# Input loads of an encoder block in a new order: x first, constants on the second queue, tiles 4 to 7 reordered

## The chip, the core and the metric

One NeuronCore of a Trainium2 chip runs the whole program. It has TensorE (PE, matrix products and transposes), VectorE (DVE), ScalarE (ACT), GpSimd (POOL) and SyncE (SP), which run side by side and meet at semaphores only. Loads are started by SP or ACT, each on a queue of its own, and are carried out by the same 16 DMA engines. The metric is the device time of one execution in microseconds; the time of a kernel is the median of its runs.

## The reference

One layer of an encoder in float32: 512 tokens, width 1024, hidden width 2816. The part at the start, which the change touches, is this (cut from the reference):

```python
c_act = jax.nn.silu(c)
mods = jnp.split(c_act @ w_ada[l] + b_ada[l], N_MOD, axis=-1)
sh1, sc1, g1, sh2, sc2, g2, sh3, sc3, g3 = mods
h = modulate(rmsnorm(x, norm_g[l, 0]), sh1, sc1)     # y * (1 + scale) + shift
x = x + 0.5 * g1[:, None, :] * swiglu(h, w_ffn1_in[l], w_ffn1_out[l])
```

Then come a mixer (a bidirectional HGRN2 group and a windowed attention group with a relative bias from `rel_bias` and a sink logit) and a second FFN. All of it is computed from `x`, `c` and the weights.

## The kernel before

Every float32 product is made of three products of parts rounded to a narrower format: `hi_hi`, `lo_hi` and `hi_lo`, of the weights (`w_hi`, `w_lo`) and of the modulated input (`h_hi`, `h_lo`). The input is kept transposed, as 8 tiles of 128 channels by 512 tokens. A unit is 256 columns of a weight matrix, in two banks; units 0 and 1 are the gate and the up part of the first 256 hidden channels.

The start cannot wait for all of the modulation, so it is made in pieces. The scale vector of the first norm has 1024 values, each a sum of 1024 products of `cact` (silu of c) and a column of `w_ada`. Its first quarter (tiles 0 and 1) is summed by PE: `direct_sums` (L2141) multiplies `scale_in[0]` with `cact`. The second quarter (tiles 2 and 3) is summed by PE as a row (`direct_rows`, L2151), and DVE takes the diagonal (L1448). The half for tiles 4 to 7 is summed by DVE (`scale_step`, L1384), from `scale_half`, and PE adds over partitions (`column_sums`, L2133). `shift_step` does the same for the shift. `first_factor` (L1394) makes the factor of a tile; ACT then writes `h_hi` (`first_hi`, L785) and `tmod` (`first_t`, L791), and DVE writes `h_lo` (`first_lo`, L1413). The norm itself comes from squares of `x_nat` on ACT and DVE, and `turn_xn` (L2130) transposes the normed x, `turn_x` (L2127) x itself; ACT copies the latter to `xT` (`evac_x`, L781).

The order of all this is written out by hand, one list for each engine:
- SP (L519 to L552) issues loads: `c_row`, `ident` (the identity that every transpose multiplies with), the two halves of x, `sink_r`, `table`, `relb` (for the attention bias), the first scale quarter in two halves, weights of unit 0 (tiles 0 to 3) and unit 1, the second scale quarter, `scale_half`, the rest of unit 0's weights, and, once the first sums are done (`s_mm`), the shift.
- ACT (L763 to L858) issues six small loads into `rows` (L770, L772: biases, norm gains and the like), makes `cact` (L774), squares x, and works through the tiles. The weights of unit 0 are split by ACT in two parts, at L812 and, for tiles 4 to 7, at L831.
- PE (L2117 to L2266) starts with `spin` (L2112), products of ones that nobody reads, then waits for `c_row` and `ident`, transposes c, x and `rows`, makes the sink and bias products (L2174, L2175), the direct sums, and goes through `hi_hi`, `lo_hi` and `hi_lo` of units 0 and 1 in parts of two tiles.
- DVE (L1427 to L1485) squares, scales, splits weights and makes the low parts.

PE, ACT and DVE each take their list in order; a wait in it holds all that is behind it.

Of the kernel before, what the change touches and what calls it, by code (L numbers as in the profile page):

```python
# [28 lines left out]
P = 128  # L29
TOK = 512  # L30
D = 1024
DT = D // P
# [76 lines left out]
def build(nc, x, c, w_ada, b_ada, norm_g, w_ffn1_in, w_ffn1_out, w_ffn2_in, w_ffn2_out,  # L109
# [163 lines left out]
    with ctx:  # L273
# [119 lines left out]
        def as_f32(ap):  # L393
            return ap.bitcast(f32)
# [91 lines left out]
        def _(sp):  # L486
            wa = w_ada[0].rearrange("(k p) m -> p k m", p=P)

            def load_scale(q, piece):
                sp.dma_start(scale_in[q][:, 4 * piece:4 * piece + 4, :],  # L490
                             wa[:, 4 * piece:4 * piece + 4, D + 2 * P * q:D + 2 * P * (q + 1)]
                             ).then_inc(first_ready[2 * q + piece], 16)
# [26 lines left out]
            sp.dma_start(c_row[:], c.rearrange("o (t q) -> (o t) q", q=P)).then_inc(consts_loaded, 16)  # L519
            sp.dma_start(ident[:], ident_c.ap()).then_inc(consts_loaded, 16)  # L520
            for half in range(2):
                sp.dma_start(x_nat[:, 2 * half:2 * half + 2, :],
                             x[0].rearrange("(t p) d -> p t d", p=P)[:, 2 * half:2 * half + 2, :]
                             ).then_inc(x_loaded[half], 16)
            sp.dma_start(sink_r[:], attn_sink).then_inc(bias_consts, 16)
# [3 lines left out]
            load_scale(0, 0)  # L529
            load_scale(0, 1)  # L530
            load_w(0, slice(0, 4), first_ready[6])
            load_w(1, everything, raw_ready[1])
            load_scale(1, 0)
            load_scale(1, 1)
# [3 lines left out]

            sp.wait_ge(s_mm, 1)
# [208 lines left out]
        def _(a):  # L748
# [11 lines left out]
            for f in ffns:  # L760

                a.sem_inc(f.silu, 1 if f.r else 2)
            a.wait_ge(pool_set, 3)  # L763
# [17 lines left out]
            def evac_x(d):  # L781
                a.wait_ge(x_tr, d + 1)
                sc.activation(xT[:, d, :], bank[X_BANK[d]][:], ACT.Copy).then_inc(xT_act, 1)

            def first_hi(d):  # L785
                a.wait_ge(xn_tr, d + 1)
                a.wait_ge(fac_done[0], (1, 1, 2, 2, 3, 3, 3, 3)[d])
                sc.activation(h_hi[:, d, :], bank[XN_BANK[d]][:], ACT.Copy, scale=fac[:, 0, d:d + 1]
                              ).then_inc(norms[0].hi, 1)

            def first_t(d):  # L791

                a.wait_ge(norms[0].lo, d + 1)
                sc.activation(tmod[:, d, :], bank[XN_BANK[d]][:], ACT.Copy, scale=fac[:, 0, d:d + 1]
                              ).then_inc(norms[0].t, 1)
# [5 lines left out]
            a.wait_ge(vec_step, 1)  # L801
            sc.activation(vec[:], bank[0][:, 0:P], ACT.Copy).then_inc(vec_step, 1)
            square(2)
            a.wait_ge(xsq_done, TT)
            sc.activation(rms0[:, 1, :], rms0[:, 0, :], ACT.Sqrt, bias=eps_t[:], scale=1.0 / D).then_inc(norms[0].rt, 1)
            a.wait_ge(norms[0].rinv, 1)
            sc.activation(xn[:, 0, :], x_nat[:, 0, :], ACT.Copy, scale=rms0[:, 2, 0:1]).then_inc(norms[0].rt, 1)
            evac_x(0)
            a.wait_ge(bias_mm, 1)
            sc.activation(row8[:], bank[3][0:QH, :], ACT.Copy).then_inc(rowpad_done, 1)  # L810
# [16 lines left out]
            a.dma_start(bias_rows.rearrange("(h j) -> h j", h=QH), row8[:]).then_inc(bias_stored, 16)  # L827
            evac_x(3)
            evac_x(4)
            a.wait_ge(raw_ready[0], 16)  # L830
            sc.activation(w_hi[0][:, 4 * 2 * P:], w_first[0][:, 4 * 2 * P:], ACT.Copy).then_inc(whi_done, 1)  # L831
            first_hi(4)
            first_hi(5)
            first_t(4)
            first_hi(6)
# [412 lines left out]
        def _(v):  # L1248
# [121 lines left out]
            def first_step(step, out, chunk, k, first=0):  # L1370

                if k == first:
                    ins = ve.tensor_scalar(out, chunk, cact[:, k:k + 1], None, ALU.mult)
                else:
                    v.wait_ge(s_step, step + k - first)
                    ins = ve.scalar_tensor_tensor(out, chunk, cact[:, k:k + 1], out, ALU.mult, ALU.add)
                ins.then_inc(s_step, 1)
# [6 lines left out]
            def scale_step(k):  # L1384
                if k % 4 == 0:
                    v.wait_ge(first_ready[4 + k // 4], 16)
                first_step(16, scale_acc[:], scale_half[k // 4][:, k % 4, :], k)
# [41 lines left out]
            v.wait_ge(vec_step, 2)  # L1429
            ve.tensor_scalar(modv[:, DT:2 * DT], vec[:, DT:2 * DT], 1.0, None, ALU.add).then_inc(lb_dve, 1)  # L1430
# [4 lines left out]
            for t in range(1, TT):  # L1435
                ve.tensor_scalar(xn[:, t, :], x_nat[:, t, :], rms0[:, 2, t:t + 1], None, ALU.mult).then_inc(xn_done, 1)
            v.wait_ge(lb_dve, 1)
# [7 lines left out]
            ve.tensor_tensor(w_lo[1][:], w_first[1][:], as_f32(w_hi[1][:]), ALU.subtract).then_inc(wlo_done, 1)  # L1445
            v.wait_ge(s_mm, 2)
# [3 lines left out]
            v.wait_ge(s_step, 15)  # L1450
            ve.tensor_reduce(quarter_acc[0][:, 0:2], diagonal, AX.X, ALU.add).then_inc(s_step, 1)
            v.wait_ge(s_step, 16)
# [3 lines left out]
            v.wait_ge(c_step, 2)  # L1456
            for k in range(3):
                scale_step(k)
            for k in range(3, DT):
                scale_step(k)  # L1460
# [577 lines left out]
        def _(pe):  # L2038
# [102 lines left out]
            def direct_sums(q, piece):  # L2141

                pe.wait_ge(first_ready[2 * q + piece], 16)
                for i in range(2):
                    for k in range(4 * piece, 4 * piece + 4):
                        ins = te.matmul(SCALE_SUMS[2 * q + i], scale_in[q][:, k, i * P:(i + 1) * P],
                                        cact[:, k:k + 1].to_broadcast([P, P]), start=(k == 0), stop=(k == DT - 1))
                if piece == 1:
                    ins.then_inc(s_mm, 1)
# [10 lines left out]
            spin(4)  # L2160
# [4 lines left out]
            spin(3)  # L2165
            pe.wait_ge(rows_loaded, 16 * 6)
            te.transpose(bank[0][:, 0:P], rows[:], ident[:]).then_inc(vec_step, 1)
            spin(1)
# [3 lines left out]
            pe.wait_ge(pool_set, 7)  # L2172
            pe.wait_ge(bias_consts, 48)
            te.matmul(SINK_SUM, ones[0:1, :], sink_r[:], start=True, stop=True).then_inc(sink_step, 1)  # L2174
            te.matmul(bank[3][0:QH, :], relb[:], table[:], start=True, stop=True).then_inc(bias_mm, 1)  # L2175
            pe.wait_ge(vec_step, 2)
            direct_sums(0, 0)
            direct_sums(0, 1)
            pe.wait_ge(norms[0].rt, 2)
            pe.wait_ge(xn_done, 3)  # L2180
            for d in range(3):
                turn_xn(d)
# [54 lines left out]
            hi_lo(1, (2, 3)).then_inc(first_used, 1)  # L2237
# [3 lines left out]
            column_sums(24, scale_acc, 4)  # L2241
            pe.wait_ge(xT_act, 5)
# [3 lines left out]
            for tiles in ((4, 5), (6, 7)):  # L2246
                if tiles[0] == 6:
                    pe.wait_ge(norms[0].t, 5)
                    turn_xn(7)
                hi_hi(0, tiles)  # L2250
                pe.wait_ge(wlo_done, 2)
                lo_hi(0, tiles)
                ins = hi_lo(0, tiles)
            ins.then_inc(stage_done, 1)
# [453 lines left out]
```

## Time and profile before

| | us |
|---|---|
| median of 3 runs | 1030.61 (1030.56 to 1030.64) |
| the profiled execution | 1030.24 |
| its span | 1028.4 |
| PE busy | 1020.9 (99%) |
| DVE busy | 801.9 (78%) |
| ACT busy | 507.3 (49%) |

The profile is one execution. Times are from the start of its span. A row of a timeline has the start, the time taken, the engine, the line of the kernel, the operation with its tiles, how many instructions were merged, and in brackets the idle time before it with what ended that. The profiled execution is 1.8 us longer than its span.

### The profile page before, as it was taken

Reading aid. Unit: us, or ns where it says so; the run is one execution under the profiler, and the core shown is the slowest. Engines: PE = TensorE matmul, PEld = TensorE weight load, DVE = VectorE, ACT = ScalarE, POOL = GpSimd, SP = SyncE. Lnnn points to the kernel's source line nnn. Section 1 sums busy time; section 2 is a strip of 40 time slices with the busy share of each in tenths; the row PEclk is TensorE's granted clock in tenths of the full one; section 3 lists DMA queues with packets and bytes.
Section 4 is the critical chain, followed back from the end, with each engine's and each line's share of the span. In section 5 each row is a group of like instructions: output and inputs, shape, how many; then the busy total and the mean of one; then the engine's idle time right before and its main releaser. Section 6 shows DMA issues by size and latency. Waiting matters only on the chain.

```text
span 1028.4 us, 16817 instructions
## 1 busy us (share of the span) xinstructions
PE 1020.9 (99%) x6298; PEld 905.6 (88%) x6298; DVE 801.9 (78%) x1175; ACT 507.3 (49%) x782; POOL 44.5 (4%) x32
## 2 busy tenths in 40 slices
PE   9999999999999999999999999999999999999998
PEld 7788999999888888888888898888999999988886
DVE  4989899988987789878888549878988888746433
ACT  5546555555322354682535773454655555532231
POOL 0000000000000150000200000420000000000000
PEclk9999999999999999999999999999999999999999
DMA  9643443444877442922121031222233232364312
GB/s 346 235 164 126 141 136 109 127 138 151 295 268 249 147 164 87 281 82 83 41 72 32 1 83 42 84 80 83 101 105 113 91 122 82 123 245 132 113 41 82
DMA packets 93810, 133.59 MB, mean 130 GB/s; under 512 B 10785, under 2 KB 77213, under 8 KB 93638
## 3 DMA queue, kind: packets, MB, share of 16 engines
q1 hardware_dynamic: 93438, 130.83, 38.1%
q10 hardware_dynamic: 328, 2.17, 0.6%
q8 instruction: 28, 0.46, 0.2%
q14 instruction: 16, 0.13, 0.0%
HBM read 130.88 MB, written 4.21 MB: 131 GB/s over the span
## 4 chain that ended last, share of the span: by engine, by line
PE 91%; DVE 6%; ACT 1%; issue 1%; DMA 0%; ACTq 0%; DVEq 0%
PE bank L2043 15%; PE bank L2044 14%; PE bank L2045 14%; PE bank L2320 11%; PE bank L2319 11%; PE bank L2318 11%; PE bank L2422 2%; PE bank L2523 2%; PE bank L2616 1%; DVE w_lo L1255 1%; PE bank L2509 1%; PE bank L2206 1%; PE bank L2192 1%; PE bank L2198 1%; DVE tmod L1339 1%; PE bank L2498 1%
## 5 line engine op out<-in xcount | busy, mean ns | idle before, releaser
L758 ACT ACTIVATE w_hi<-w_raw 128x2048 fp32r<-128x2048 f32 x47 | 89.9, 1913 | 202.7 <-PE bank L2045 191.1
L1255 DVE TENSOR_TENSOR w_lo<-w_raw,w_hi 128x2048 fp32r<-128x2048 f32 x47 | 109.5, 2329 | 94.0 <-ACT w_hi L758 93.9
L2318 PE MATMUL bank<-t_hi,left_hi 128*128 128x256 f32 x544 | 154.0, 283 | 0.0
L2319 PE MATMUL bank<-t_lo,left_hi 128*128 128x256 f32 x544 | 154.0, 283 | 0.0
L2320 PE MATMUL bank<-t_hi,left_lo 128*128 128x256 f32 x544 | 153.9, 283 | 0.0
L2043 PE MATMUL bank<-a_hi,w_hi 128*128 128x512 f32 x352 | 137.7, 391 | 0.3 <-DVE w_lo L1255 0.3
L2045 PE MATMUL bank<-a_hi,w_lo 128*128 128x512 f32 x352 | 137.0, 389 | 0.0
L2044 PE MATMUL bank<-a_lo,w_hi 128*128 128x512 f32 x352 | 137.0, 389 | 0.0
L2043 PE MATMUL bank<-h_hi,w_hi 128*128 128x512 f32 x336 | 133.3, 397 | 0.2
L2045 PE MATMUL bank<-h_hi,w_lo 128*128 128x512 f32 x336 | 130.9, 390 | 0.0
L2044 PE MATMUL bank<-h_lo,w_hi 128*128 128x512 f32 x336 | 130.9, 389 | 0.0
L2319 PE MATMUL bank<-h_lo,left_hi 128*128 128x256 f32 x408 | 115.5, 283 | 0.0
L2320 PE MATMUL bank<-h_hi,left_lo 128*128 128x256 f32 x408 | 115.5, 283 | 0.0
L2318 PE MATMUL bank<-h_hi,left_hi 128*128 128x256 f32 x408 | 115.5, 283 | 0.0
L927 ACT ACTIVATE left_hi<-s_raw 128x512 fp32r<-128x512 f32 x136 | 85.7, 630 | 54.0 <-PE bank L2320 29.9
L2318 PEld LDWEIGHTS bank<-t_hi,left_hi 128*128 128x128 f32 x544 | 104.4, 192 | 0.0
L2319 PEld LDWEIGHTS bank<-t_lo,left_hi 128*128 128x128 f32 x544 | 104.4, 192 | 0.0
L2320 PEld LDWEIGHTS bank<-t_hi,left_lo 128*128 128x128 f32 x544 | 104.4, 192 | 0.0
L1547 DVE TENSOR_TENSOR left_lo<-s_raw,left_hi 128x512 fp32r<-128x512 f32 x136 | 92.8, 685 | 5.1 <-ACT left_hi L927 3.8
L1547 DVE TENSOR_TENSOR left_lo<-w_raw,left_hi 128x512 fp32r<-128x512 f32 x102 | 67.4, 687 | 21.0 <-ACT left_hi L927 19.9
L2043 PEld LDWEIGHTS bank<-a_hi,w_hi 128*128 128x128 f32 x352 | 66.1, 188 | 14.3 <-DVE w_lo L1255 0.7
L2318 PEld LDWEIGHTS bank<-h_hi,left_hi 128*128 128x128 f32 x408 | 78.3, 192 | 0.1
(318 smaller groups left out, 1914.5 us busy)
## 6 DMA issues: line engine op xcount, KB each, us to landing
w_raw<-in_w_ffn_in SPq DMA_DIRECT2D x42, 1024.0 KB, 4.9
ada<-in_w_ada SPq DMA_DIRECT2D x24, 1024.0 KB, 5.0
w_raw<-in_w_ffn_out SPq DMA_DIRECT2D x22, 1024.0 KB, 4.8
w_raw<-in_w_mix_in SPq DMA_DIRECT2D x11, 1024.0 KB, 5.1
shift_in<-in_w_ada SPq DMA_DIRECT2D x4, 1024.0 KB, 9.9
ada_row<-in_w_ada SPq DMA_DIRECT2D x8, 512.0 KB, 4.2
x_nat<-in_x SPq DMA_DIRECT2D x2, 1024.0 KB, 6.1
scale_in<-in_w_ada SPq DMA_DIRECT2D x4, 512.0 KB, 7.9
```

Of the source, the lines that this page charges most:

```text
L758: sc.activation(w_hi[n % 2][:], src[:], ACT.Copy).then_inc(whi_done, 1)
L927: sc.activation(left_hi[p][:], left_source(f, u, p), ACT.Copy).then_inc(high_done, 1)
L1255: ve.tensor_tensor(w_lo[n % 2][:], src[:], as_f32(w_hi[n % 2][:]), ALU.subtract).then_inc(wlo_done, 1)
L1547: ve.tensor_tensor(left_lo[p][:], left_source(f, u, p), as_f32(left_hi[p][:]), ALU.subtract).then_inc(low_done, 1)
L2043: te.matmul(out_ap, wh, xh, start=first, stop=False)
L2044: te.matmul(out_ap, wh, xl, start=False, stop=False)
L2045: return te.matmul(out_ap, wl, xh, start=False, stop=last)
L2318: te.matmul(into, wh, xh[:, k, :], start=(opens and k == 0), stop=False, skip_group_check=True)
L2319: te.matmul(into, wh, xl[:, k, :], start=False, stop=False, skip_group_check=True)
L2320: ins = te.matmul(into, wl, xh[:, k, :], start=False, stop=(k == 3), skip_group_check=True)
L2422: ins = te.matmul(bank[4 + h][:, cols].rearrange("p (m two j) -> p m two j", two=2, j=b), kc(lev, h // GH)[:, h % GH, cols], alternate(q_b ...
L2523: ins = te.matmul(bank[4 + 2 * (n % 2) + g][:, j * (DH + 1):(j + 1) * (DH + 1)], pT[u % 4][:, i, :], av[:, key_first(n) + i, g, :], start= ...
```

## The change

On SP the first half of x goes first, then the three small loads for the bias, then the second half of x. `c_row` and `ident` are issued by ACT, ahead of its loads into `rows`. The first scale quarter is loaded in three pieces (tiles 0 and 1, 2 and 3, 4 to 7), and `direct_sums` takes them as they come, tile by tile. `scale_half` and what follows it are issued once the first sums are done. PE makes the bias and sink products right after the first half of x is transposed, transposes `rows` after the second half, and does seven spins where it did ten. ACT and DVE take the copy of `rows` (`vec`, `modv`) and the copy of the bias rows at other places. DVE does two steps of the scale half ahead of the diagonal. For tiles 4 to 7 ACT splits the weights ahead of its two xT copies and writes `h_hi` 6 ahead of `tmod` 4; PE makes the column sums ahead of `hi_lo(1, (2, 3))` and transposes xn 7 ahead of `hi_lo(0, (4, 5))`. What is computed is the same.

```diff
@@ -486,10 +486,8 @@
         def _(sp):
             wa = w_ada[0].rearrange("(k p) m -> p k m", p=P)
 
-            def load_scale(q, piece):
-                sp.dma_start(scale_in[q][:, 4 * piece:4 * piece + 4, :],
-                             wa[:, 4 * piece:4 * piece + 4, D + 2 * P * q:D + 2 * P * (q + 1)]
-                             ).then_inc(first_ready[2 * q + piece], 16)
+            def load_scale(q, tiles, ready):
+                sp.dma_start(scale_in[q][:, tiles, :], wa[:, tiles, D + 2 * P * q:D + 2 * P * (q + 1)]).then_inc(ready, 16)
 
             def load_scale_half(piece):
                 sp.dma_start(scale_half[piece][:], wa[:, 4 * piece:4 * piece + 4, D + TOK:2 * D]
@@ -516,27 +514,29 @@
                 sp.dma_start(dst[:, tiles, :], ffns[0].w_in[:, tiles, col:col + 2 * P]).then_inc(ready, 16)
 
             everything = slice(0, DT)
-            sp.dma_start(c_row[:], c.rearrange("o (t q) -> (o t) q", q=P)).then_inc(consts_loaded, 16)
-            sp.dma_start(ident[:], ident_c.ap()).then_inc(consts_loaded, 16)
-            for half in range(2):
+            def load_x(half):
                 sp.dma_start(x_nat[:, 2 * half:2 * half + 2, :],
                              x[0].rearrange("(t p) d -> p t d", p=P)[:, 2 * half:2 * half + 2, :]
                              ).then_inc(x_loaded[half], 16)
+
+            load_x(0)
             sp.dma_start(sink_r[:], attn_sink).then_inc(bias_consts, 16)
             sp.dma_start(table[:], table_c.ap()).then_inc(bias_consts, 16)
             sp.wait_ge(pool_set, 5)
             sp.dma_start(relb[0:NB, :], rel_bias).then_inc(bias_consts, 16)
-            load_scale(0, 0)
-            load_scale(0, 1)
+            load_x(1)
+            load_scale(0, slice(0, 2), first_ready[4])
+            load_scale(0, slice(2, 4), first_ready[0])
+            load_scale(0, slice(4, DT), first_ready[1])
             load_w(0, slice(0, 4), first_ready[6])
             load_w(1, everything, raw_ready[1])
-            load_scale(1, 0)
-            load_scale(1, 1)
+            load_scale(1, slice(0, 4), first_ready[2])
+            load_scale(1, slice(4, DT), first_ready[3])
+
+            sp.wait_ge(s_mm, 1)
             load_scale_half(0)
             load_scale_half(1)
             load_w(0, slice(4, DT), raw_ready[0])
-
-            sp.wait_ge(s_mm, 1)
             load_shift(0, 0)
             load_shift(0, 1)
 
@@ -760,6 +760,8 @@
             for f in ffns:
 
                 a.sem_inc(f.silu, 1 if f.r else 2)
+            a.dma_start(c_row[:], c.rearrange("o (t q) -> (o t) q", q=P)).then_inc(consts_loaded, 16)
+            a.dma_start(ident[:], ident_c.ap()).then_inc(consts_loaded, 16)
             a.wait_ge(pool_set, 3)
             sc.activation(warm[:, 1:2], eps_t[:], ACT.Silu)
             a.wait_ge(pool_set, 5)
@@ -798,16 +800,16 @@
                 sc.activation(h_hi[:, d, :], tmod[:, d, :], ACT.Identity, bias=modv[:, d:d + 1]).then_inc(norms[0].hi, 1)
 
             square(0)
-            a.wait_ge(vec_step, 1)
-            sc.activation(vec[:], bank[0][:, 0:P], ACT.Copy).then_inc(vec_step, 1)
+            a.wait_ge(bias_mm, 1)
+            sc.activation(row8[:], bank[3][0:QH, :], ACT.Copy).then_inc(rowpad_done, 1)
             square(2)
             a.wait_ge(xsq_done, TT)
             sc.activation(rms0[:, 1, :], rms0[:, 0, :], ACT.Sqrt, bias=eps_t[:], scale=1.0 / D).then_inc(norms[0].rt, 1)
+            a.wait_ge(vec_step, 1)
+            sc.activation(vec[:], bank[5][:, 0:P], ACT.Copy).then_inc(vec_step, 1)
             a.wait_ge(norms[0].rinv, 1)
             sc.activation(xn[:, 0, :], x_nat[:, 0, :], ACT.Copy, scale=rms0[:, 2, 0:1]).then_inc(norms[0].rt, 1)
             evac_x(0)
-            a.wait_ge(bias_mm, 1)
-            sc.activation(row8[:], bank[3][0:QH, :], ACT.Copy).then_inc(rowpad_done, 1)
             a.wait_ge(first_ready[6], 16)
             sc.activation(w_hi[0][:, 0:4 * 2 * P], w_first[0][:, 0:4 * 2 * P], ACT.Copy).then_inc(first_split, 1)
             first_hi(0)
@@ -825,14 +827,14 @@
             first_t(3)
             a.wait_ge(rowpad_done, 1)
             a.dma_start(bias_rows.rearrange("(h j) -> h j", h=QH), row8[:]).then_inc(bias_stored, 16)
+            a.wait_ge(raw_ready[0], 16)
+            sc.activation(w_hi[0][:, 4 * 2 * P:], w_first[0][:, 4 * 2 * P:], ACT.Copy).then_inc(whi_done, 1)
             evac_x(3)
             evac_x(4)
-            a.wait_ge(raw_ready[0], 16)
-            sc.activation(w_hi[0][:, 4 * 2 * P:], w_first[0][:, 4 * 2 * P:], ACT.Copy).then_inc(whi_done, 1)
             first_hi(4)
             first_hi(5)
+            first_hi(6)
             first_t(4)
-            first_hi(6)
             first_t(5)
             first_hi(7)
             first_t(6)
@@ -1383,8 +1385,8 @@
 
             def scale_step(k):
                 if k % 4 == 0:
-                    v.wait_ge(first_ready[4 + k // 4], 16)
-                first_step(16, scale_acc[:], scale_half[k // 4][:, k % 4, :], k)
+                    v.wait_ge(first_ready[4 + k // 4], 16 if k else 32)
+                first_step(14 if k < 2 else 16, scale_acc[:], scale_half[k // 4][:, k % 4, :], k)
 
             def shift_step(half, k):
                 if k % 4 == 0:
@@ -1426,14 +1428,14 @@
 
             v.sem_inc(s_step, 14)
             square(1)
-            v.wait_ge(vec_step, 2)
-            ve.tensor_scalar(modv[:, DT:2 * DT], vec[:, DT:2 * DT], 1.0, None, ALU.add).then_inc(lb_dve, 1)
             square(3)
             v.wait_ge(norms[0].rt, 1)
             ve.reciprocal(rms0[:, 2, :], rms0[:, 1, :]).then_inc(norms[0].rinv, 1)
             v.wait_ge(norms[0].rinv, 1)
             for t in range(1, TT):
                 ve.tensor_scalar(xn[:, t, :], x_nat[:, t, :], rms0[:, 2, t:t + 1], None, ALU.mult).then_inc(xn_done, 1)
+            v.wait_ge(vec_step, 2)
+            ve.tensor_scalar(modv[:, DT:2 * DT], vec[:, DT:2 * DT], 1.0, None, ALU.add).then_inc(lb_dve, 1)
             v.wait_ge(lb_dve, 1)
             v.wait_ge(s_mm, 1)
             first_factor((0, 1), [sums[:, 0:1] for sums in SCALE_SUMS[0:2]])
@@ -1443,20 +1445,20 @@
             first_lo(1)
             v.wait_ge(whi_done, 1)
             ve.tensor_tensor(w_lo[1][:], w_first[1][:], as_f32(w_hi[1][:]), ALU.subtract).then_inc(wlo_done, 1)
+            v.wait_ge(c_step, 2)
+            scale_step(0)
+            scale_step(1)
             v.wait_ge(s_mm, 2)
             diagonal = quarter_acc[1][:].rearrange("p (i q) -> p i q", i=2)
             ve.tensor_tensor(diagonal, SCALE_ROWS.rearrange("p (i q) -> p i q", i=2),
                              ident[:].unsqueeze(1).to_broadcast([P, 2, P]), ALU.mult).then_inc(s_step, 1)
-            v.wait_ge(s_step, 15)
+            v.wait_ge(s_step, 17)
             ve.tensor_reduce(quarter_acc[0][:, 0:2], diagonal, AX.X, ALU.add).then_inc(s_step, 1)
-            v.wait_ge(s_step, 16)
+            v.wait_ge(s_step, 18)
             first_factor((2, 3), (quarter_acc[0][:, 0:1], quarter_acc[0][:, 1:2]))
             first_lo(2)
             first_lo(3)
-            v.wait_ge(c_step, 2)
-            for k in range(3):
-                scale_step(k)
-            for k in range(3, DT):
+            for k in range(2, DT):
                 scale_step(k)
             shift_step(0, 0)
             v.wait_ge(s_mm, 3)
@@ -2138,15 +2140,14 @@
                                     start=True, stop=True)
                 ins.then_inc(s_mm, 1)
 
-            def direct_sums(q, piece):
-
-                pe.wait_ge(first_ready[2 * q + piece], 16)
-                for i in range(2):
-                    for k in range(4 * piece, 4 * piece + 4):
-                        ins = te.matmul(SCALE_SUMS[2 * q + i], scale_in[q][:, k, i * P:(i + 1) * P],
+            def direct_sums(tiles, ready):
+
+                pe.wait_ge(ready, 16)
+                for k in tiles:
+                    for i in range(2):
+                        ins = te.matmul(SCALE_SUMS[i], scale_in[0][:, k, i * P:(i + 1) * P],
                                         cact[:, k:k + 1].to_broadcast([P, P]), start=(k == 0), stop=(k == DT - 1))
-                if piece == 1:
-                    ins.then_inc(s_mm, 1)
+                return ins
 
             def direct_rows(piece):
 
@@ -2157,27 +2158,27 @@
                 if piece == 1:
                     ins.then_inc(s_mm, 1)
 
-            spin(4)
+            spin(3)
             pe.wait_ge(x_loaded[0], 16)
             turn(bank[1], x_nat, 0, (0, 1))
             pe.wait_ge(c_step, 2)
             turn(bank[2], x_nat, 1, (0, 1))
-            spin(3)
-            pe.wait_ge(rows_loaded, 16 * 6)
-            te.transpose(bank[0][:, 0:P], rows[:], ident[:]).then_inc(vec_step, 1)
-            spin(1)
+            pe.wait_ge(pool_set, 7)
+            pe.wait_ge(bias_consts, 48)
+            te.matmul(bank[3][0:QH, :], relb[:], table[:], start=True, stop=True).then_inc(bias_mm, 1)
+            te.matmul(SINK_SUM, ones[0:1, :], sink_r[:], start=True, stop=True).then_inc(sink_step, 1)
+            spin(2)
             pe.wait_ge(x_loaded[1], 16)
             turn(bank[1], x_nat, 0, (2, 3)).then_inc(x_tr, 1)
             turn(bank[2], x_nat, 1, (2, 3)).then_inc(x_tr, 1)
-            pe.wait_ge(pool_set, 7)
-            pe.wait_ge(bias_consts, 48)
-            te.matmul(SINK_SUM, ones[0:1, :], sink_r[:], start=True, stop=True).then_inc(sink_step, 1)
-            te.matmul(bank[3][0:QH, :], relb[:], table[:], start=True, stop=True).then_inc(bias_mm, 1)
-            pe.wait_ge(vec_step, 2)
-            direct_sums(0, 0)
-            direct_sums(0, 1)
+            pe.wait_ge(rows_loaded, 16 * 6)
+            te.transpose(bank[5][:, 0:P], rows[:], ident[:]).then_inc(vec_step, 1)
+            direct_sums(range(2), first_ready[4])
+            direct_sums(range(2, 4), first_ready[0])
+            direct_sums(range(4, DT), first_ready[1]).then_inc(s_mm, 1)
             pe.wait_ge(norms[0].rt, 2)
             pe.wait_ge(xn_done, 3)
+            pe.wait_ge(vec_step, 2)
             for d in range(3):
                 turn_xn(d)
 
@@ -2234,24 +2235,24 @@
             turn_xn(4)
             hi_hi(1, (2, 3))
             lo_hi(1, (2, 3))
-            hi_lo(1, (2, 3)).then_inc(first_used, 1)
             pe.wait_ge(norms[0].t, 4)
             turn_x(3)
             turn_x(4)
             column_sums(24, scale_acc, 4)
+            hi_lo(1, (2, 3)).then_inc(first_used, 1)
             pe.wait_ge(xT_act, 5)
             turn_xn(5)
             turn_xn(6)
             pe.wait_ge(whi_done, 2)
-            for tiles in ((4, 5), (6, 7)):
-                if tiles[0] == 6:
-                    pe.wait_ge(norms[0].t, 5)
-                    turn_xn(7)
-                hi_hi(0, tiles)
-                pe.wait_ge(wlo_done, 2)
-                lo_hi(0, tiles)
-                ins = hi_lo(0, tiles)
-            ins.then_inc(stage_done, 1)
+            hi_hi(0, (4, 5))
+            pe.wait_ge(wlo_done, 2)
+            lo_hi(0, (4, 5))
+            pe.wait_ge(norms[0].t, 5)
+            turn_xn(7)
+            hi_lo(0, (4, 5))
+            hi_hi(0, (6, 7))
+            lo_hi(0, (6, 7))
+            hi_lo(0, (6, 7)).then_inc(stage_done, 1)
             hi_hi(1, (4, 5))
             pe.wait_ge(norms[0].t, 7)
             turn_x(5)
```

## Rows read from the trace of the kernel before

**Rows 1.** The page: busy time of PE; the chain that ended last, by engine.
```profile
PE 1020.9 (99%) x6298; PEld 905.6 (88%) x6298; DVE 801.9 (78%) x1175; ACT 507.3 (49%) x782; POOL 44.5 (4%) x32
...
PE 91%; DVE 6%; ACT 1%; issue 1%; DMA 0%; ACTq 0%; DVEq 0%
```

**Rows 2.** The chain of waits from 0 to 18 us: start, duration, what.
```profile
0.87 1.28 ACT L764
...
3.86 5.02 DMA rows<-in_qk_norm_g
...
10.44 0.95 PE bank L2175 x2
11.39 3.77 PE bank L2146 x32
...
16.55 1.21 PE bank L2192 x4
```

**Rows 3.** PE's timeline of the start.
```profile
3.14 0.27 PE L2120 MATMUL bank<-ident,c_row 8*128 8x8 f32 x1
3.34 3.62 PE L2115 MATMUL bank<-ones 128*128 128x256 f32 x8
...
7.25 1.46 PE L2115 MATMUL bank<-ones 128*128 128x256 f32 x6
```

**Rows 4.** PE's timeline at tiles 4 to 7, and one row of ACT's.
```profile
34.19 1.09 PE L2124 MATMUL bank<-ident,xn 128*128 128x128 f32 x8
35.80 1.21 PE L2192 MATMUL bank<-h_hi,w_hi 128*128 128x512 f32 x4 [0.52 <-ACT h_hi L788]
...
40.08 0.73 PE L2192 MATMUL bank<-h_hi,w_hi 128*128 128x512 f32 x2 [0.31 <-ACT h_hi L788]
...
33.05 1.08 ACT L783 ACTIVATE xT<-bank 128x512 f32<-128x512 f32 x2 [5.33 <-PE bank L2124]
```

**Rows 5.** Timelines of the queues of SP and ACT: issues of loads and stores.
```profile
0.74 0.41 SPq L519 DMA_DIRECT2D c_row<-in_c  x1
...
1.61 0.93 SPq L522 DMA_DIRECT2D x_nat<-in_x  x2
...
2.23 0.31 ACTq L770 DMA_DIRECT2D rows<-in_norm_g  x1
...
27.03 0.28 ACTq L827 DMA_DIRECT2D bias_rows<-row  x1
```

**Rows 6.** ACT's timeline: the first reader of x.
```profile
6.73 1.06 ACT L779 ACTIVATE xn<-x_nat 128x1024 f32<-128x1024 f32 x1 [0.82 <-DMA x_nat<-in_x]
```

**Rows 7.** Packets by queue (q1 SP, q10 ACT): 2.0-2.9, 2.9-5.9, 5.9-6.3, 6.35-6.95, 29.9-31.0 us.
```profile
q10 hardware_dynamic: 84, 0.04, 14.2%
...
q1 hardware_dynamic: 236, 0.97, 88.0%
...
q10 hardware_dynamic: 35, 0.01, 11.7%
...
q10 hardware_dynamic: 31, 0.01, 5.9%
...
q10 hardware_dynamic: 16, 0.02, 4.2%
```

**Rows 8.** Issue to landing, of SP's loads issued at 2.08, 4.30, 12.45 and 15.24 us.
```profile
DMA to landing us min/median/max: 7.1/7.1/7.1
...
DMA to landing us min/median/max: 7.8/7.8/7.8
...
DMA to landing us min/median/max: 9.0/9.0/9.0
...
DMA to landing us min/median/max: 11.5/11.5/11.5
```

**Rows 9.** DVE's timeline: the diagonal and the steps of the scale half.
```profile
23.50 0.42 DVE L1448 TENSOR_TENSOR quarter_acc<-bank,ident 128x256 f32<-128x256 f32 x1 [1.83 <-PE bank L2155]
...
27.42 5.54 DVE L1376 SCALAR_TENSOR_TENSOR scale_acc<-scale_half,cact,scale_acc 128x512 f32<-128x512 f32 x7
```

## Prediction

> **What bounds the kernel now.** I read the page first: TensorE (PE) is busy for 99% of the span and carries 91% of the chain that ended last [rows 1]. So only what lets PE start its real work earlier, or closes a hole between its instructions, shortens anything. The chain of waits comes next [rows 2]. Its first long link is no arithmetic: the small vectors that ACT loads into `rows` arrive at 8.9 us (3.86 + 5.02). Then PE transposes them, the bias product takes 0.95 us, the 32 instructions of the direct sums 3.77 us, to 15.16, and the first FFN product starts at 16.55 us, after twelve transposes. PE's timeline [rows 3] shows that before 6.8 us it does little but `spin` products, whose result nobody reads. After 16.55 PE is fully fed up to 50 us, but for two holes at 35.80 and 40.08 us [rows 4]. All later work follows from semaphores of this work, so a start earlier by d ends the kernel d earlier, as long as no load becomes late.
>
> The profiled execution took 1030.24 us for a span of 1028.4. The median of the runs shown is 1030.61, 0.37 more; I work on the execution and add 0.37 at the end.
>
> **Part 1: loads and the start.** The first half of `x` is now SP's first issue, at 0.74 instead of 1.61 us [rows 5]. It landed at 6.73 [rows 6]; 0.87 earlier is 5.86. The loads behind it run at the full rate of the queue, so they move by about the same 0.87, in spite of the three tiny loads in between (67 KB; at the 0.97 MB in 3 us of [rows 7] that is 0.2 us). Now the second half of `x` (issue 2.08, 7.1 to landing) comes at 9.2 and the second half of the first scale quarter (issue 4.30, 7.8 to landing) at 12.1 [rows 8]; they come at about 8.55 and 11.25.
>
> `c_row` and `ident` pay for this: they move to ACT's queue and are issued behind x in time, `ident` at about 1.3 us (ACT starts at 0.87 [rows 2], and the small issue of `c_row` takes 0.41 [rows 5]). Nothing on PE goes without `ident`: every transpose reads it, and PE waits for both ahead of its second group of spins. What does a small load on ACT's queue cost when a 1 MB load of SP's is ahead? Two cases are in the trace. `norm_g` and four more loads were issued on ACT's queue from 2.23 us on [rows 5]. Between 2.9 and 5.9 us the engines moved 236 packets, and all were SP's; ACT's queue comes back with 35 packets between 5.9 and 6.3, when the first half of x is through [rows 7]. And the store of `bias_rows`, issued at 27.03 [rows 5], has its 16 packets (0.02 MB, all of it) only after 29.9, when SP's backlog ends [rows 7]. Against that stands the first stretch, 2.0 to 2.9 us: with no big load ahead, 84 packets of ACT's queue passed. The bounds for `ident` are thus 3.14 us, as now [rows 3], and the landing of x and a little, 5.86 + 0.3 = 6.15. I take the second, since `norm_g` is the nearest row: same queue, same load ahead, and x now leads by some 0.5 us.
>
> The Trainium skill, page "DMA: Bandwidth & Descriptors", section "Issuing engines are not separate DMA queues", says that loads issued by different engines run on the same 16 DMA engines and interleave, and that a second issuing engine saves only the time to issue. By that rule the move can buy no more than the 0.87 us of issue time. The same page ("Queues, rings and completion order") lets each DMA engine drain one packet of a ring before it turns to another ring. If a packet is a single row of x, `ident` is early (rival A); if it is all rows of one engine, `ident` is late. The trace agrees with the second in 2.9 to 5.9 us, and with the first in 6.35 to 6.95.
>
> With `ident` at 6.15 PE's start is, step by step: transpose of c_row 0.27, to 6.4 [rows 3]. Six spin instructions: now the eight from 3.34 take 3.62 us, 0.45 each, and the six from 7.25 take 1.46, 0.24 each [rows 3]; that is the 1.2 and the 2.4 GHz level. PE has a pause from 3.2 to 6.15, so I take the lower level again: 2.6 us, to 9.0. Four transposes of x at twice 0.11 (the eight of [rows 4] from 34.19 start 0.11 apart): 0.9, to 9.9. By then PE has done as much unbroken work as stood before the clock rose now (3.34 to 6.8), so the rest goes at the upper level: bias product 0.95, to 10.85 [rows 2]; sink product 0.3, to 11.15; four spin instructions 0.9, to 12.05; four transposes 0.45 and that of `rows` 0.2, to 12.7; direct sums 3.77, to 16.45; then 1.39 as now from the last sum (15.16) to the first product (16.55) [rows 2]: 17.85. That is 1.3 us lost. ACT is not later: silu of c at 6.45, a table load of 1.28 [rows 2] to 7.9, warm-up and a square of 1.06 [rows 6] to 9.3; from the bias product at 10.85 three operations of 1024 columns at 1.06 and three small ones at half of it, 4.8 us, to 15.7; then it waits for the sums.
>
> **Part 2: what is moved at no price.** The finer scale pieces keep the sums at 3.77 us; they only let them start sooner. `scale_half` now waits on SP for the first sums; behind it are the last weight half and both shift loads. Now its first load is issued at 12.45 and lands 9.0 later, at 21.45 [rows 8]. DVE's two early `scale_step`s (0.79 each by 5.54 / 7) stand in its 1.83 us of waiting ahead of the diagonal at 23.50 [rows 9]. Issued at 16.5, with the backlog still running, it lands by about 21.5, and DVE asks at 21.67 + 1.3 = 23: nothing. Without that cover the diagonal, and with it tiles 2 and 3, would be late by as much as the load. The later `vec` copy and `modv` have no reader before the sums: nothing.
>
> **Part 3: tiles 4 to 7.** At 33.05 ACT does two xT copies, then the weight split, then h_hi 4 [rows 4]. PE's eight transposes from 34.19, 0.11 apart, are through at 35.1, and its next product starts at 35.80: a hole of 0.7 (0.52 of it seen as idle). With the split ahead of the copies it falls into ACT's idle 5.33 us, as its weights are there (issue 15.24, 11.5 to landing, 26.7 [rows 8]). The column sums go ahead of `hi_lo(1, (2, 3))`, so the factors come 0.92 sooner; their input ends at 32.96 now [rows 9], but with two of its steps done early some 1.2 sooner. Next, h_hi 6 goes ahead of tmod 4, and turn_xn(7) ahead of the last `hi_lo(0, (4, 5))`; that gives ACT 0.9 us more for h_hi 7 and closes the hole at 40.08, idle 0.31 [rows 4] and, as with the first, about 0.25 more from start to start: 0.56. Next late would be w_lo of the second half and h_lo 4 on DVE, with some 0.3 us to spare. Sum: 0.7 + 0.56 = 1.26 us gained, between 0.6 (one hole comes back) and 1.3.
>
> **Sum.** +1.3 - 1.26 = 0.0: 1030.3 for the execution, 1030.6 as a median. Its own range is 1029.8 to 1032.0: `ident` 0.3 sooner or later, the clock up late (at most 0.9 on bias product and spins), one hole left.
>
> **Rivals.** (A) `ident` passes between the rows of x and lands at 3.2 to 4.3 us. For it: 31 packets of ACT's queue passed beside the second half of x after 6.35 us [rows 7]. Against it: `norm_g`. Then x is turned from 6.1 on, bias product and spins are through by 8.75, x's second half is there at 8.55, `rows` by about 9.3, and the sums end at 13.45 instead of 15.16. That is 1.7 less (1.0 with `ident` at 4.3), with part 3 2.96 (2.2): 1027.65 to 1028.4.
>
> (B) is my forecast.
>
> (C) `ident` comes only behind the second half of x too, as `bias_rows` came only when SP's backlog was gone. Then it lands at 8.8 instead of 6.15, and all of PE's work up to the sums moves by that 2.65, less 0.25 for waits that vanish: +2.4, 1033.0. It makes the kernel slower by over 0.2% from `ident` at about 8.4 us on. Against it: ACT's 35 packets passed between the two halves, and the second half is now issued at 2.3, a microsecond behind `ident`.
>
> (D) The new order in part 3 closes no hole, since ACT and DVE take turns in any order there: B with 1.26 more, 1031.9; with A, 1028.9.
>
> **How the numbers follow.** A 0.30, B 0.48, C 0.10, D 0.12 (a third of it with A). Likeliest is B: 1030.6. To hold 8 in 10 the range takes in most of A and of D: 1027.5 to 1032.4. A measurement of this kernel can tell about 0.2%, 2.1 us, from no change. Faster by more: nearly all of A, 0.28; slower by more: C and the tail of D, 0.13; within: 0.59.
>
> **What would show it.** The first square of x at about 5.9 us instead of 6.73 (order of loads). The transpose of c_row: near 6.1 for B, below 4.3 for A, near 8.8 for C. The first L2192 product: 17.9, 14.9 or 20.3. The spins behind it at 0.45 or 0.24 us each. No idle time of PE ahead of h_hi 4 and 7, and 18.55 us from the first FFN product to the first one of tile 4 in unit 0, instead of 19.25 (16.55 to 35.80 [rows 2, 4]); at the next hole the whole 1.26. DVE's diagonal not waiting for `scale_half`. I am wrong if PE starts its sums before 12 us, or if the distance from there to the end is other than 1.26 shorter.

## The result: the start is as forecast in one half of the runs, and up to 4.3 us later in the other

| | median us | runs | range |
|---|---|---|---|
| before, in the same runs | 1030.39 | 20 | 1030.11 to 1030.92 |
| changed | 1031.95 | 20 | 1030.11 to 1034.69 |

The ratio is 1.0017, with a 95% interval of 1.0011 to 1.0023: slower, by 1.6 us. But the median of the changed kernel lies where hardly a run does. Its 20 runs stand in three groups: ten at 1030.1 to 1030.9, five at 1033.0 to 1033.4, five at 1034.3 to 1034.7. The old kernel's 20 runs make one group, 0.8 us wide. In the series below it ran 72 times more; 71 of these runs lie in 1030.0 to 1030.8, and one took 1032.29 us. No trace of that one was kept.

The profiled execution (1030.40 us, span 1028.6) is of the first group. Its chain of waits from 0 to 20 us (start, duration, what), as [rows 2] for before:

```profile
1.52 4.60 DMA ident<-identity_const
...
6.43 2.86 PE bank L2117 x6
9.29 0.85 PE bank L2126 x4
10.14 0.97 PE bank L2168 x2
...
13.04 3.57 PE bank L2148 x32
16.61 1.31 PE bank L2126 x12
...
18.01 1.22 PE bank L2193 x4
```

`ident` is now the first long link, where the vectors in `rows` were. It is issued at 1.52 and takes 4.60 us to land. The first FFN product starts at 18.01 instead of 16.55 us. The PE timeline of the same execution shows the pause, and that later no hole is left where [rows 4] had two:

```profile
6.16 0.27 PE L2122 MATMUL bank<-ident,c_row 8*128 8x8 f32 x1 [2.95 <-DMA ident<-identity_const]
...
36.50 1.32 PE L2193 MATMUL bank<-h_hi,w_hi 128*128 128x512 f32 x4
...
42.68 1.08 PE L2193 MATMUL bank<-h_hi,w_hi 128*128 128x512 f32 x4
```

From the first FFN product to the first product of unit 1's tiles (4, 5) it is 42.68 - 18.01 = 24.67 us. Before, that product came at 42.50, so it was 25.95. The start lost 1.46, the order of tiles 4 to 7 gave back 1.28, and what is left, 0.18, is the 0.16 between the two profiled executions.

The packets of the two queues (q1 is SP's, q10 ACT's; packets, MB, share of the engines) in 2.6 to 5.0 and 5.0 to 6.0 us say why `ident` is late:

```profile
q1 hardware_dynamic: 232, 0.95, 97.9%
q10 hardware_dynamic: 16, 0.00, 0.8%
...
q1 hardware_dynamic: 158, 0.27, 70.0%
q10 hardware_dynamic: 245, 0.11, 37.8%
```

While the first half of x passes, ACT's queue moves 16 packets; once it is through, 245 in one microsecond. It is the picture of `norm_g` in [rows 7]. So far the changed kernel should equal the old one. What follows is about the other half of the runs.

### The profile page after: what moved, and what is told of

Read it like the earlier page. It is cut to its first block, busy times and chain, and to the rows that moved or that the text cites. A ratio compares the mean times of both kernels' runs of the same rounds, so it can differ in the third digit from the quotient of the medians.

```text
span 1028.6 us, 16805 instructions
## 1 busy us (share of the span) xinstructions
PE 1019.2 (99%) x6292; PEld 904.7 (88%) x6292; DVE 802.0 (78%) x1175; ACT 507.7 (49%) x782; POOL 44.3 (4%) x32
## 4 chain that ended last, share of the span: by engine, by line
PE 92%; DVE 6%; ACT 1%; issue 1%; DMA 0%; ACTq 0%; DVEq 0%
PE bank L2045 15%; PE bank L2047 14%; PE bank L2046 14%; PE bank L2321 11%; PE bank L2320 11%; PE bank L2319 11%; PE bank L2423 2%; PE bank L2524 2%; PE bank L2617 1%; DVE w_lo L1257 1%; PE bank L2510 1%; PE bank L2207 1%; PE bank L2193 1%; PE bank L2199 1%; DVE tmod L1341 1%; PE bank L2499 1%
## 5 line engine op out<-in xcount | busy, mean ns | idle before, releaser
L2320 PEld LDWEIGHTS bank<-h_lo,left_hi 128*128 128x128 f32 x408 | 78.3, 192 | 0.1
```

The costliest lines, as they stand in the source:

```text
L2320: te.matmul(into, wh, xl[:, k, :], start=False, stop=False, skip_group_check=True)
```

## The experiments

A profile shows the length of PE's instructions, and from it the level of its clock: a spin instruction (128x256) takes 634 ns at the lower level and 379 ns at the upper one, and starts 0.43 or 0.22 us after the one before it.

Two theories stood against each other for the three groups. Theory 1: after its pause PE's clock comes up at a moment that differs from run to run, and all work until then takes twice as long. Theory 2: some load of the new order lands late in some runs. Runs of one experiment share the runs of the old kernel beside them; those stood at 1030.38 us (33 runs), 1030.40 (24) and 1030.25 (15).

**The changed kernel again, three times.** No edit.

> The changed kernel, nothing edited, timed again. Its runs so far stood in three groups (about 1030.4, 1033.1 and 1034.5 us), and the profile is of the first group. Theory 1 (PE's clock): the groups come from the moment at which PE's clock rises to the upper level, 10.2 us in the profile at hand; a run of a slow group shows the spins, the bias product and perhaps the direct sums at twice the duration, and the first FFN product at 20.8 or 22.1 us instead of 18.0. Theory 2 (loads): the groups come from ident, the vectors in rows or the scale pieces landing late in some executions; a slow run then shows idle time of PE ahead of a transpose or a sum, with the durations unchanged. Both expect groups again.

Of 11 runs nine stood at 1030.09 to 1030.79 us and two at 1032.83 and 1033.26; the profile is of the first kind. The ratio of this series is 1.0006 [0.9997, 1.0015]. How many runs fall above the first group differs from series to series (10 of 20, then 2 of 11), and with it the verdict on the kernel.

> The changed kernel once more, nothing edited, for a profile of one of its slower executions (10 in 20 of its first runs, 2 in 11 of the next stood 2.7 or 4.1 us above the fastest). Clock theory: if it is a slower one, PE's instructions up to the sums take twice as long for 2.8 or 4.1 us more than now, and no load lands later. Loads theory: the durations are as now and an idle time is longer.

This one came out at 1034.3 us (span 1032.5), in the slowest group. Its chain of waits, against the one above:

```profile
1.52 4.56 DMA ident<-identity_const
...
6.12 0.27 PE bank L2122
6.39 2.86 PE bank L2117 x6
9.25 0.85 PE bank L2126 x4
10.11 1.80 PE bank L2168 x2
...
12.43 2.00 PE bank L2117 x4
14.43 0.85 PE bank L2126 x4
...
15.50 5.02 PE bank L2148 x32
20.52 1.31 PE bank L2126 x12
...
21.92 1.21 PE bank L2193 x4
```

Up to 10.1 us the two agree link by link, `ident` included, and there is no new wait anywhere. Then the same instructions take longer: the bias product 1.80 instead of 0.97, the four spin instructions 2.00 instead of 1.06, four transposes 0.85 instead of 0.44, the sums 5.02 instead of 3.57. The sums tell where it ends (one line of the kernel, in 15.3 to 18.2 and in 18.5 to 20.4 us; durations in ns):

```profile
L2148 PE MATMUL bank<-cact,scale_in x14: 421/421/421, 15.3 to 18.1; 128*128 128x128 f32 x14
...
L2148 PE MATMUL bank<-cact,scale_in x18: 273/273/347, 18.3 to 20.2; 128*128 128x128 f32 x18
```

The clock rose between 18.1 and 18.4 us, in the middle of the sums. In the 1030.40 us execution it rose at the start of the bias product, at 10.1 to 10.2. The clock record kept with the two traces says the same: its first entry, at the full level, stands at 18.42 us of the span in the one and at 10.16 in the other. Theory 1 explains all of the 3.9 us (21.92 against 18.01), theory 2 none. Later the executions run alike: from 21.92 us to unit 1's tiles (4, 5) it is 24.67 us again.

> The changed kernel once more, unedited, for a profile of the group between, at 1033.1 us. Clock theory: if it is of that group, the clock rises later than in the 1030.4 us profile (10.2 us) and earlier than in the 1034.3 us one (where the direct sums begin at the lower level), and the first FFN product comes at about 20.7 us.

This was 1030.99 us, so not the group between. Its chance was of another kind: `ident` landed 0.55 us later, and the first FFN product came at 18.65.

```profile
6.71 0.27 PE L2122 MATMUL bank<-ident,c_row 8*128 8x8 f32 x1 [3.49 <-DMA ident<-identity_const]
...
18.65 1.22 PE L2193 MATMUL bank<-h_hi,w_hi 128*128 128x512 f32 x4
```

So a load does land at varying times, as theory 2 says, but that is worth 0.6 us here. The clock rose at 10.9 us, during the bias product; in the profile of the 11 runs above (1030.21 us) it rose at 9.6, during the transposes of x. No trace of the group at 1033 us was caught; that its clock rose between the two is argued, not shown.

**PE kept busy until ident lands.** No load touched.

```diff
-            spin(2)
+            spin(6)
             pe.wait_ge(consts_loaded, 32)
```

> The changed kernel with six spins instead of two ahead of the wait for c_row and ident, so that PE works until ident lands at 6.1 us. Nothing else is edited, ident is as late as before. Theory 1: the clock is up when ident lands or soon after, the transposes, bias product and spins behind it run at the upper level, the first product comes at about 16.2 us, and the groups vanish: 1028.5 in all runs. Theory 2: 1030.4 at best, with groups as before.

1028.66 us, 11 runs, all in 1028.54 to 1029.18; the ratio to the old kernel is 0.9984 [0.9975, 0.9993]. With four spins more, whose result nobody reads, no run stands in an upper group, and the slowest of them is faster than the fastest of the changed kernel (1030.09 us): the change has turned into a gain. The loads are those of the changed kernel. The median is the expected time; the first product came at 16.85 in the profile, where 16.2 was expected, since the spins themselves ended only at 6.56, and the clock rose only during the three behind them, at 7.3 us:

```profile
1.14 5.49 PE L2117 MATMUL bank<-ones 128*128 128x256 f32 x12 [1.14 <-POOL eps_t L696]
6.56 0.27 PE L2122 MATMUL bank<-ident,c_row 8*128 8x8 f32 x1
6.76 1.81 PE L2117 MATMUL bank<-ones 128*128 128x256 f32 x6
```

**The constants back on SP, ahead of x.**

```diff
+            sp.dma_start(c_row[:], ...)
+            sp.dma_start(ident[:], ...)
             load_x(0)
...
-            a.dma_start(c_row[:], ...)
-            a.dma_start(ident[:], ...)
```

> Undoes one part: c_row and ident are issued by SP again, ahead of x; all else as in the changed kernel. Theory 1: ident lands at 3.1 us, PE works from there without a pause, the clock rises early enough for all that matters, and all runs stand in one group. The first product comes at about 15.6 us (x's second half at 9.4, sums from 10.1, last scale piece at 12.3 and 16 instructions more to 14.2, then 1.39), with 1.26 us from tiles 4 to 7: 1030.4 - 0.95 - 1.26 = 1028.2. Theory 2, if it is the finer scale pieces or the vectors in rows that land late: the groups stay, 2.7 and 4.1 us apart.

The best run is 1028.47, as expected, and its profile has `ident` at 3.14 us. But the groups did not go: 1028.47 to 1028.67 (2 runs), 1029.64 to 1029.91 (4), 1031.14 to 1031.52 (5), median 1029.91. So theory 1's forecast for this kernel failed: I had taken the pause for `ident` as the only one that matters. No slower run of this kernel has a trace, but the mean granted clock of each run goes with its time: 1.000 for the two fast ones, 0.998 for the four between, 0.996 to 0.999 for the five above. PE's list here still has waits of its own ahead of x and of the bias product:

```profile
3.34 2.93 PE L2117 MATMUL bank<-ones 128*128 128x256 f32 x6
6.82 0.66 PE L2126 MATMUL bank<-ident,x_nat 128*128 128x128 f32 x4 [0.55 <-DMA x_nat<-in_x]
7.75 1.01 PE L2168 MATMUL bank<-table,relb 33*8 33x512 f32 x2 [0.28 <-DMA relb<-in_rel_bias]
```

The old kernel had four spins there and none of this idle time [rows 3]. Whether it is that, or the loads, the next one tells.

**The same, with more spins.** `spin(3)` ahead of the first half of x is `spin(4)`, and `spin(2)` ahead of the second half is `spin(4)`.

> As the one with the constants on SP, with four spins instead of three behind the transpose of c_row and four instead of two ahead of the second half of x: they fill the waits of that kernel's PE (0.55 us ahead of 6.82, 0.3 ahead of 7.75, some up to 9.98). Clock theory: its three groups (1028.5, 1029.8 and 1031.3 us) come from work at the lower clock after 6.8 us, and with the waits filled nearly all runs come to 1028.5 to 1028.8. Rival (loads): the groups stay as they are, since no load is touched.

1029.05 us, 11 runs, all in 1028.67 to 1029.36; ratio 0.9986 [0.9977, 0.9995]. The groups above 1029.6 are gone and no load was touched. The last spins end at 10.7, some 0.5 us after x's second half has landed, and hold up its transposes by that much. But not every wait was filled in the profile:

```profile
3.38 3.02 PE L2117 MATMUL bank<-ones 128*128 128x256 f32 x8
7.00 0.66 PE L2126 MATMUL bank<-ident,x_nat 128*128 128x128 f32 x4 [0.61 <-DMA x_nat<-in_x]
```

The clock rose during the eight spin instructions, which took 3.02 us instead of the 3.62 of [rows 3], and so a pause of 0.61 us stands ahead of x here too. What the spins changed is that PE works on until x if the clock is still low; that it was the pause of 0.55 us which made the groups is not shown.

**The price of the order of tiles 4 to 7.** As with the constants on SP, and on ACT, PE the old order: the two xT copies ahead of the weight split, `first_t(4)` ahead of `first_hi(6)`, the column sums behind `hi_lo(1, (2, 3))`, `turn_xn(7)` ahead of `hi_hi(0, (6, 7))`.

> As the one with the constants on SP, and the order of tiles 4 to 7 is the old one too (weight split behind the two xT copies, tmod 4 ahead of h_hi 6, column sums behind hi_lo of tiles 2 and 3, turn_xn(7) ahead of hi_hi of tiles 6 and 7). It prices part 3 by itself, without the pause at the start. My sum says 1.26 us slower than the one with the new order, 1029.5; rival D says no difference.

One of the 11 runs took 3575.15 us, for which the record has no reason. The median of the other ten is 1031.83, against 1029.91 of the kernel with the new order; but medians say little here, as both kernels fall into groups. The lowest runs are 1029.81 and 1028.47, and the spans of the two profiles 1028.0 and 1026.7: 1.3 us. The holes are back:

```profile
35.43 1.21 PE L2193 MATMUL bank<-h_hi,w_hi 128*128 128x512 f32 x4 [0.52 <-ACT h_hi L790]
...
39.70 0.73 PE L2193 MATMUL bank<-h_hi,w_hi 128*128 128x512 f32 x2 [0.31 <-ACT h_hi L790]
...
42.11 1.07 PE L2193 MATMUL bank<-h_hi,w_hi 128*128 128x512 f32 x4
```

Its first FFN product is at 16.15 us, so the distance is 25.96; in the kernel with the new order it is 24.64 (16.06 to 40.70).

**x behind the small loads.** `c_row` and `ident` stay on ACT's queue; `load_x(0)` stands behind the three bias loads, ahead of `load_x(1)`.

> The changed kernel with the first half of x issued behind the three small bias loads instead of ahead of them (at about 1.9 instead of 0.75 us); c_row and ident stay on ACT's queue. It tells what holds ident up. If it is the 1 MB of x that stands in front: ident is now ahead of x and lands at about 3.3 us, x at 6.9. If it is ACT's queue as such: ident lands at 6.1 or later again.

`ident` came at 3.60 us instead of 6.16, on the same queue:

```profile
3.60 0.27 PE L2122 MATMUL bank<-ident,c_row 8*128 8x8 f32 x1 [0.38 <-DMA ident<-identity_const]
...
7.17 0.68 PE L2126 MATMUL bank<-ident,x_nat 128*128 128x128 f32 x4 [0.45 <-DMA x_nat<-in_x]
...
15.81 1.22 PE L2193 MATMUL bank<-h_hi,w_hi 128*128 128x512 f32 x4
```

So it is the megabyte of x in front, and not the second queue, that held `ident` up. The time is 1028.46 us, ratio 0.9987 [0.9976, 0.9997]. The eight runs are not one group: five stand at 1028.10 to 1028.51, and three at 1029.67 to 1030.25. PE has pauses of 0.38 and 0.45 us here and no spins more, and these runs were made in the same series as those of the kernel with the constants on SP and more spins, which has no upper group.

**The old kernel with a pause.** The four spins between c_row and x are left out of the kernel before; nothing else is edited.

```diff
-            spin(4)
             pe.wait_ge(x_loaded[0], 16)
```

> The kernel before with one edit: the four spins between the transpose of c_row (3.1 us) and the arrival of x (6.7 us) are left out, so PE stands idle there. Loads, order and all else are those of before. Clock theory: groups appear in the old kernel too. The best runs stay at 1030.4 (the clock is up by the time of the sums), others come 1 to 5 us later, with the bias product, spins and sums at the lower level. Rival (it is the new order of loads or of PE's list that makes the groups): nothing changes, since spins are work that nobody reads: 1030.4 in all runs.

1032.26 us, 11 runs, 1031.09 to 1032.69, ratio 1.0017 [1.0008, 1.0026]. The ratio is that of the change, made by leaving out idle work alone. There are no groups as in the changed kernel, though: the runs spread over 1.6 us. I had expected the best runs at 1030.4, and none of them comes to it. In the profile (1032.23 us) the transposes and the next spins, after a pause of 3.65 us, go at the lower level, and the first FFN product comes at 18.54 instead of 16.55:

```profile
7.07 1.11 PE L2124 MATMUL bank<-ident,x_nat 128*128 128x128 f32 x4 [3.65 <-DMA x_nat<-in_x]
7.98 2.77 PE L2115 MATMUL bank<-ones 128*128 128x256 f32 x6
...
18.54 1.21 PE L2191 MATMUL bank<-h_hi,w_hi 128*128 128x512 f32 x4
```

**Spins ahead of ident only.** As the kernel that spins until ident, and without the `spin(3)` behind the transpose of c_row.

> As the one that spins until ident lands (six spins ahead of the wait for c_row and ident), and without the three spins behind the transpose of c_row. Clock theory: the unbroken work now stands ahead of ident, so the three spins behind it are not needed; x is transposed at about 6.8 us, the bias product is through at 8.1, the second half of x at 8.9 sets the sums at 9.4 to 13.2, and ACT's chain (table load to 8.2, squares, root, xn, weight split to about 14.6) sets the first product at 15.3: 1027.3 us, in one group. Rival: the clock needs the spins behind ident too, then groups come back, the faster one at 1027.3 and others up to 4 us above.

1027.83 us, 8 runs in 1027.44 to 1028.25, ratio 0.9974 [0.9963, 0.9984]: the best version, 0.3% below the old kernel, in one group. In the profile the clock rose during the twelve spin instructions (they took 4.45 us, where those of the kernel with six spins ahead took 5.49 at the lower level), and everything behind `ident` runs at the upper level:

```profile
1.14 4.45 PE L2117 MATMUL bank<-ones 128*128 128x256 f32 x12 [1.14 <-POOL eps_t L696]
6.21 0.23 PE L2122 MATMUL bank<-ident,c_row 8*128 8x8 f32 x1 [0.62 <-DMA ident<-identity_const]
6.37 0.77 PE L2126 MATMUL bank<-ident,x_nat 128*128 128x128 f32 x4
...
15.67 1.22 PE L2192 MATMUL bank<-h_hi,w_hi 128*128 128x512 f32 x4
```

The first product comes at 15.67, where 15.3 was expected.

Of one kernel 10 in 20 runs and then 2 in 11 stood in the upper groups, so that none in 11 would say little by itself. All kernels together say more: the three with added spins have no run in an upper group in 30, while the three with pauses beside them have 2 in 11, 9 in 11 and 3 in 8 (the changed kernel, the constants on SP, x behind the small loads).

## Why the prediction was wrong

**What held.** The load order: `ident` behind x, forecast to be ready at 6.15 us, released PE at 6.16; the reason given for it (norm_g in [rows 7]) is the one that the kernel with x behind the small loads confirms, and rivals A and C fall with it. The Trainium skill's "DMA: Bandwidth & Descriptors" ("Issuing engines are not separate DMA queues") says that loads of different issuing engines share the same DMA engines, and that a second issuing engine saves only the time to issue. The trace agrees: `ident`, issued by a second engine, landed at 6.12 us, behind the first half of x, which DVE read from 5.64 on. How much of one load a DMA engine takes in before it turns to another no run shows. The first FFN product was forecast for 17.85 and came at 18.01, the sums for 16.45 and ended at 16.61. Part 3 was forecast at 1.26 us and measured 1.28 in the changed kernel and 1.3 by itself, so rival D falls. `scale_half` held nothing up: DVE's two early steps ran at 23.04, and even in the 1034.3 us execution, where SP issued it only after 20 us, the later distance was the same 24.67. The profiled execution was forecast at 1030.3 and took 1030.40.

**What failed** is one step of part 1: "By then PE has done as much unbroken work as stood before the clock rose now (3.34 to 6.8), so the rest goes at the upper level." I took one moment in one trace for a law, and I read that trace wrongly. The old kernel's PE did not begin its unbroken work at 3.34 us:

```profile
1.14 2.07 PE L2115 MATMUL bank<-ones 128*128 128x256 f32 x4 [1.14 <-POOL eps_t L696]
```

From 1.14 us on it had no pause until its clock was up at 6.8 [rows 3]. The changed kernel's PE does the same 2.07 us of spins and then stands idle for 2.95 us. That the forecast moment came true in the 1030.40 us execution was luck: in the 1034.3 us one PE did the very same work from 6.12 us on, and its clock stayed low until 18.3 or 18.4. I had bounded the term at 0.9 us, "the clock up late", on the bias product and the spins; by my own rows both at the lower level would already cost 0.95 and 0.9 more. Its true size is the lower level for everything up to the middle of the sums: bias and sink product, spins and transposes of x and `rows` took 5.39 us (10.11 to 15.50) instead of 2.90 (10.14 to 13.04), the sums 5.02 instead of 3.57; 3.9 us together. With half the runs at +2.7 or +4.1 the median went up by 1.6 us, to 1031.95, inside the range that I gave but not the "no change" that I forecast.

The second mistake lies under it. I forecast one time for a kernel whose time had become a distribution. The pause was in my own step list ("from 3.2 to 6.15"); whether the old kernel's spins were what kept nearly all its runs together is what I didn't ask. The old kernel with a pause answers it: without four of its spins it is 2.0 us slower at the median (1032.26 against 1030.25), and its runs spread over 1.6 us instead of 0.3.

**Still open:** what sets the moment at which the clock rises in a given run, and with it the share of runs in the upper groups, which was 10 of 20 in one series and 2 of 11 in another. The work done before the rise doesn't settle it: with the same twelve spin instructions from 1.14 us on and no pause in either, the clock rose at 4.4 us in one execution (spins ahead of `ident` only) and at 7.3 in another (PE kept busy until `ident` lands). Spins do not fix the moment; they stand where a late rise costs little.

## What to carry to other kernels

Price a wait of PE near the start of a kernel not by its length alone but also by the work behind it, which may run at twice the duration; in this case that cost up to 3.9 us more. When an edit opens such a pause, try spins in it in the same edit, and look whether they end before the awaited load lands. A small load that much depends on belongs ahead of the first large one, whatever queue it is on. When the runs of a kernel stand in groups, compare the groups and their traces; the median says only how many fell in each.

## What the hardware did that I had not expected

- The same list of PE instructions, with the same start times to 0.05 us up to 10.1 us, came to the upper clock level at 10.1 us in one execution and in the middle of the sums, after 18.1 us, in another.
- The mean granted clock does not show it: it reads 0.999 to 1.000 for runs of all three groups of the changed kernel. In the 1034.3 us execution the view by stretches reads 1.00 (the column after POOL's) in a stretch where every PE instruction took the longer duration:

```profile
10.00:14.00 4.00, 4.00 (x9) 1.97 (x9) 0.61 (x3) 1.92 (x4) 0.00 (x0) 1.00 1.09 385
```

  The trace's clock record has its first entry at 18.42 us, and what lies before it reads as full. At the start of a kernel the durations of equal instructions tell the level.

- Kernels with short pauses only also had groups. With `ident` at 3.14 us, and pauses of 0.55 and 0.28 us in the profile, runs spread over 1028.5 to 1031.5; with three spins more in PE's list over 1028.7 to 1029.4. Whether the length of a pause or its place decides is not shown.
